# Four token norms: statistics as columns, spread by TensorE, and two row copies moved to ScalarE

## The chip, the cores and the metric

The kernel runs on one core of a Trainium2 chip. The metric is the time of one execution on the device in microseconds. Three runs of the kernel before gave 3365.01, 3369.65 and 3364.98 us, median 3365.01 us.

## What is computed

Two transformer blocks run one after the other on 512 tokens of 1024 channels, in float32. The first block has two layers: modulated RMS norm, input projection, global and window attention, short convolution, a gated merge, and an expert-choice feed-forward layer of 16 experts. Its first layer carries 256 context tokens beside the 512, so its vectors are 768 long. The second block has one layer: dilated and latent attention, a gated mix, and a feed-forward layer of width 4096 with squared ReLU. This case is about the RMS norms:

```python
def rms_norm(x, g):
    xf = x.astype(jnp.float32)
    y = xf * lax.rsqrt(jnp.mean(xf * xf, axis=-1, keepdims=True) + EPS)
    return (y * g.astype(jnp.float32)).astype(x.dtype)
...
        h = h + rms_norm(mix, norm_mix_post)
        hn = rms_norm(h, norm_mlp_pre)
        ff = jnp.square(jax.nn.relu(hn @ w_ff1)) @ w_ff2
        h = h + rms_norm(ff, norm_mlp_post)
```

## The kernel before, in words

Activations lie transposed: channels over the 128 partitions in eight tiles (`XT[:, k, :]`, k = 0 to 7), tokens along the free dimension. A norm therefore sums squares over partitions, which TensorE does: ScalarE squares tile k, and TensorE multiplies an all-ones 128x128 matrix with it, so that every partition of a PSUM tile holds the sum for each token. Float32 matmuls stand in the trace as two MATMUL and two LDWEIGHTS records each. `act_rstd` then takes Ln of that row in PSUM (L882) and Exp of -0.5 times it (L884) into the SBUF tile `rst`, 512 or 768 tokens wide. Ln and Exp stand in different tables, so a table load goes ahead of each. VectorE multiplies every tile by its gain and by `rst` (`scalar_tensor_tensor`).

Each engine has its own program in one fixed order, with semaphore waits between them. There are four PSUM tiles of 1024 float32 columns. `bank.take` hands them out in turn; `hold` and `back` keep one out of the turn. The norms that the change touches:

- **n1**, between layer 0 and layer 1, 768 tokens (L1045 reads it). TensorE adds the last squares in `pe_squares_tail` (L844): one tile by itself, then a total that GpSimd has summed, then a last pair that VectorE has summed. ScalarE has loaded the Ln table ahead (L2232). VectorE computes scaled tiles (L1045), ScalarE their rounded part (L1029), VectorE the remainder (L1038), and TensorE starts the next projection (L657).
- **n2**, between layer 1 and the second block, 512 tokens. Four sums in `pe_squares_tail`, then Ln, Exp, `dve_split_gain` (L2349 scaled tile, L2339 rounded part, L2344 remainder), and TensorE at L636.
- **no**, the norm of the mixer's output. `pe_total` adds a total of GpSimd (L873) and the last square (L876); then Ln and Exp. VectorE makes `X = X + norm` tile by tile in `dve_add_normed`: L2678 the scaled tile, L2671 the sum.
- **nf**, the norm ahead of the feed-forward layer. For each k, when tile k of X is there, TensorE transposes three of its 128-token blocks into the tiles `back` 0 to 2 (L2474) and adds the square of tile k (`pe_square`, L864). ScalarE squares tile k (L817) when the sum of tile k-2 is done. After the loop come Ln and Exp, eight transposes for `back` 3, and on VectorE three copies of `back` 0 to 2 out of PSUM (L2743), ahead of `dve_split_gain`. ScalarE copies `back` 3 later (L2637). Then the 32 units of the first feed-forward matrix run (L636) and the second (L2494), to the end.

Two forms that the change uses elsewhere are already in the kernel. The very first norm (n0) spreads columns to rows: `e.matmul(ps[...], RC[:, c:c + 1].broadcast_to([128, 128]), ident)` at L1005. The choice of experts turns a row into columns: a 128x128 slice of `rst` as the stationary operand against one column of the identity, at L1717. The end of the kernel takes Sqrt of a column and VectorE's reciprocal (L2650 to L2660, L2766).

Of the kernel before, what the change touches and what calls it, by code (L numbers as in the profile page):

```python
# [18 lines left out]
KD = 8  # L19
# [227 lines left out]
def build(nc, I, cst, cmask, crope, at, out):  # L247
    ctx = ExitStack()
    with ctx:
# [782 lines left out]
        def dve_split_mod(e, l, ks, between=None):  # L1032
            m, X = MD[l], WX[l]

# [6 lines left out]
            for k in ks:  # L1041
                if k > 1:
                    e.wait_ge(*d_xl.at(X.key, "mod", k - 2, 1))
                for w, (a, b) in enumerate(segs(T0)):
                    e.scalar_tensor_tensor(out=raw2[k % 2][:, a:b], in0=XT[:, k, a:b], scalar=A1v[:, l, 0, k, w:w + 1], in1=rst[:, a:b],  # L1045
# [118 lines left out]
        def dve_proj(e, l, norm):  # L1164
            X = WX[l]
            if l:
                e.wait_ge(*d_mod.at("mod", 3 * l, "A"))
                e.wait_ge(*n_rs.at(norm))
# [820 lines left out]
        def pe_back(e, l, p, norm=None):  # L1989
# [166 lines left out]
        def pe_experts(e, l):  # L2156
# [53 lines left out]
        def act_experts(e, l):  # L2210
# [21 lines left out]
            e.activation(sm[:, 16:17], eps[:, 0:1], ACT.Ln, bias=eps[:, 0:1]).then_inc(*n_ln.up(st, "set"))  # L2232
# [7 lines left out]
            act_rstd(e, f"n{l + 1}", KD, T, D)  # L2240
# [44 lines left out]
        def dve_experts(e, l):  # L2285
# [16 lines left out]
            dve_low(e, WX[l + 1], 0)  # L2302

# [37 lines left out]
        def dve_split_gain(e, stage, base):  # L2341
# [4 lines left out]
            for k in range(KD):  # L2346
                if k > 1:
                    e.wait_ge(*d_xl.at(stage, k - 2))
                e.scalar_tensor_tensor(out=runs(raw2[k % 2][:, 0:NX]), in0=X_(k), scalar=colB(base + k), in1=runs(rst[:, 0:NX]),  # L2349
# [55 lines left out]
        def pe_second(e):  # L2405
# [58 lines left out]
            pe_total(e, "no", KD, NX, tmp[:, 2304:2816], sqr[0])  # L2464
            pe_norm_take(e, "nf")

            def back_take(c):
                ps, when = bank.take(("back", c), c_out.at("fin", "back", 3) if c == 3 else d_out.at("fin", "back", c))
# [18 lines left out]
            for f in range(32):  # L2487
                pe_linear3(e, X2, ("f1", f), 128, NX, ("x2", "f1", f), c_ev.at("x2", "f1", f), low=(lambda k: d_xl.at("ffgain", k)) if f == 0 else None)
# [531 lines left out]
```

## Time and profile before

| what | value |
|---|---|
| median of three runs | 3365.01 us |
| the profiled execution, its own time | 3363.93 us |
| its span, first to last instruction | 3362.0 us |
| TensorE busy | 3179.4 us, 95% |
| VectorE busy | 1400.7 us, 42% |
| ScalarE busy | 1068.3 us, 32% |
| mean granted TensorE clock | 0.983 |

The span is 1.93 us shorter than the execution's own time. A clock of 1.00 is TensorE at 2.4 GHz, 0.50 at 1.2 GHz. Busy time of TensorE is modelled for the ends of matmuls, so starts are read rather than ends where many follow each other. PEld are the weight loads of TensorE.

### The profile page before, as it was taken

What the parts mean: (1) busy time and instruction counts of PE and PEld (TensorE: products, weight loads), DVE (VectorE), ACT (ScalarE), POOL (GpSimd) and SP (SyncE); (2) the same over time, 40 slices, a digit from 0 to 9 for tenths busy, and PEclk for the clock granted to TensorE, in tenths of its full rate; (3) what the DMA queues carried; (4) which work ended last, traced back from release to release, by engine and by line L of the source; (5) the groups of instructions that cost most, each with busy time, mean ns of one, the idle gap of its engine ahead of it and who ended that gap; (6) DMA issues with size and microseconds to landing.
All of it is one profiled execution on the core that took longest, in us unless ns stands there. A gap on an engine that the chain in (4) does not pass through costs nothing.

```text
span 3362.0 us, 46341 instructions
## 1 busy us (share of the span) xinstructions
PE 3179.4 (95%) x20065; PEld 2136.8 (64%) x20065; DVE 1400.7 (42%) x2110; ACT 1068.3 (32%) x1843; POOL 278.2 (8%) x221
## 2 busy tenths in 40 slices
PE   7999999999899999999999998988889999989999
PEld 6886688888334344377678873323238757868887
DVE  4476655664201011156665541211134454453333
ACT  4715632222321211165552231100022354342323
POOL 1100100211000000011000220000002020110000
PEclk9999999999899999999999998999999999999999
DMA  8240033433999998734007649999973111323332
GB/s 233 56 128 18 1 94 107 119 102 141 336 397 365 397 348 348 250 60 133 24 17 217 193 160 377 421 421 421 422 277 94 31 50 51 95 68 99 96 100 69
DMA packets 399500, 616.91 MB, mean 183 GB/s; under 512 B 99679, under 2 KB 290497, under 8 KB 374721
## 3 DMA queue, kind: packets, MB, share of 16 engines
q1 hardware_dynamic: 393616, 597.50, 50.7%
q0 software_dynamic: 5184, 15.79, 1.4%
q8 instruction: 159, 2.61, 0.3%
q10 hardware_dynamic: 496, 0.66, 0.1%
q14 instruction: 45, 0.36, 0.0%
HBM read 606.55 MB, written 7.34 MB: 183 GB/s over the span
## 4 chain that ended last, share of the span: by engine, by line
PE 79%; DMA 8%; DVE 6%; ACT 4%; issue 1%; POOL 1%; DVEq 0%; SPq 0%; ACTq 0%; POOLq 0%
PE ps L636 32%; PE ps L2110 7%; PE ps L2494 5%; PE ps L1251 4%; PE ps L2113 3%; PE ps L2146 3%; PE ps L2106 3%; PE ps L1346 3%; PE ps L689 3%; PE ps L1528 3%; PE ps L1301 3%; DMA ring<-in_w_e_up 2%; PE ps L657 2%; PE ps L2142 2%; DMA arena<-in_w_e_down 2%; DMA ring<-in_w_e_down 2%
## 5 line engine op out<-in xcount | busy, mean ns | idle before, releaser
L636 PE MATMUL ps<-xh,wh 128*128 128x512 f32 x1912 | 634.3, 370 | 26.0 <-DVE xl L2344 10.5
L636 PE MATMUL ps<-xl,wh 128*128 128x512 f32 x1912 | 626.7, 366 | 0.0
L636 PE MATMUL ps<-xh,wl 128*128 128x512 f32 x1912 | 626.0, 365 | 0.0
L609 DVE TENSOR_TENSOR wl<-ring,wh 128x1024 fp32r<-128x1024 f32 (+1 forms) x259 | 318.6, 1231 | 305.1 <-ACT wh L600 304.5
L600 ACT ACTIVATE wh<-ring 128x1024 fp32r<-128x1024 f32 (+1 forms) x259 | 271.9, 1050 | 420.2 <-PE ps L636 167.0
L636 PEld LDWEIGHTS ps<-xh,wh 128*128 128x128 f32 x1912 | 328.4, 188 | 104.8 <-issue 26.2
L636 PEld LDWEIGHTS ps<-xh,wl 128*128 128x128 f32 x1912 | 328.4, 188 | 60.3
L636 PEld LDWEIGHTS ps<-xl,wh 128*128 128x128 f32 x1912 | 328.6, 188 | 57.9 <-issue 0.5
L2110 PE MATMUL ps<-ring,arena 128*32 128x512 f32 x1344 | 177.2, 599 | 1.0 <-ACT arena L1806 0.9
L765 DVE SCALAR_TENSOR_TENSOR tmp<-ring,cs,tmp 128x512 f32<-128x512 f32 x224 | 169.2, 803 | 1.9
L2106 PE MATMUL ps<-ring,arena 128*64 128x512 f32 x696 | 158.8, 599 | 8.1 <-DMA ring<-in_w_e_up 4.8
L1262 DVE TENSOR_REDUCE sm<-ps 128x2 f32<-128x1536 f32 (+3 forms) x96 | 142.1, 1480 | 26.1 <-PE ps L1251 25.3
L2274 DVE SCALAR_TENSOR_TENSOR y<-ps,aff,y 128x1024 fp32r<-128x1024 f32 x16 | 20.5, 1284 | 304.1 <-ACT y L2203 304.1
L1251 PE MATMUL ps<-arena 64*128 64x256 f32 (+3 forms) x800 | 143.2, 442 | 2.2 <-ACT arena L2583 2.2
L1280 ACT ACTIVATE tmp<-ps,sm 128x768 f32<-128x768 f32 (+3 forms) x176 | 132.7, 762 | 36.4 <-DVE sm L1265 25.5
L1301 PE MATMUL ps<-consts,tmp 128*128 128x128 f32 x832 | 130.5, 285 | 7.7 <-ACT tmp L1280 2.2
L1301 PEld LDWEIGHTS ps<-consts,tmp 128*128 128x128 f32 x832 | 87.5, 141 | 55.4 <-issue 26.3
L1324 DVE COPY arena<-ps 128x512 f32<-128x512 f32 (+1 forms) x136 | 86.5, 655 | 80.4 <-PE ps L1301 80.3
L2106 PEld LDWEIGHTS ps<-ring,arena 128*64 128x64 f32 x696 | 48.4, 137 | 107.9 <-issue 82.0
L2203 ACT ACTIVATE y<-ps,aff 128x1024 fp32r<-128x1024 f32 x16 | 17.8, 1115 | 308.7 <-PE ps L2152 159.4
L1599 ACT ACTIVATE tmp<-ps 128x768 f32<-128x768 f32 (+1 forms) x48 | 33.9, 706 | 254.3 <-PE ps L636 254.3
L1251 PEld LDWEIGHTS ps<-arena 64*128 64x128 f32 (+1 forms) x800 | 89.3, 187 | 34.6 <-issue 26.3
(342 smaller groups left out, 4592.9 us busy)
## 6 DMA issues: line engine op xcount, KB each, us to landing
ring<-in_w_e_up SPq DMA_DIRECT2D x86, 1024.0 KB, 14.1
ring<-in_w_e_gate SPq DMA_DIRECT2D x85, 1024.0 KB, 14.1
ring<-in_w_e_down SPq DMA_DIRECT2D x82, 1024.0 KB, 14.9
ring<-in_w_in SPq DMA_DIRECT2D x112, 512.0 KB, 4.0
arena<-in_w_e_down SPq DMA_DIRECT2D x46, 1024.0 KB, 14.8
arena<-in_w_e_gate SPq DMA_DIRECT2D x43, 1024.0 KB, 13.7
arena<-in_w_e_up SPq DMA_DIRECT2D x42, 1024.0 KB, 11.3
ring<-in_w_ada SPq DMA_DIRECT2D x80, 512.0 KB, 4.3
```

What stands on the lines that cost most here:

```text
L600: e.activation(in_heads(X, u, m.WH[:, o:o + many]), heads_of(X, u, halves.aps[s], many), ACT.Copy).then_inc(*hi.up(X.key, q))
L609: e.tensor_tensor(in_heads(X, u, m.WL[:, o:o + many]), heads_of(X, u, halves.aps[s], many), in_heads(X, u, m.WH[:, o:o + many].bitcast(F32 ...
L636: i = e.matmul(ps[0:M, a:b], w[:, k, 0:M], h[:, k, a:b], start=k == 0 and p == 0, stop=k == 7 and p == 2)
L689: i = e.matmul(ps[0:M, 0:512].rearrange("p (h t) -> p h t", h=2), w[:, k, o:o + M], aside(h, k), start=k == 0 and p == 0, stop=k == kn - 1 ...
L765: e.scalar_tensor_tensor(out=ACC[w], in0=src, scalar=csv[:, k, w:w + 1], in1=ACC[w], op0=ALU.mult, op1=ALU.add).then_inc(*d_md.up("mod", g ...
L1251: x = e.matmul(ps[:, col:col + k.shape[-1]], q, k, start=first, stop=last, skip_group_check=True)
L1262: e.tensor_reduce(mx, A.units(i, A.scores(i)), AX, ALU.max).then_inc(*a_rm.up(A.stage, i))
L1280: e.activation(dst[:, u], src[:, u], ACT.Exp, bias=A.small(i, 1)[:, u:u + 1], scale=s["scale"], accum_out=A.small(i, 2)[:, u:u + 1]).then_ ...
L1301: x = e.transpose(ps[:, 128 * c:128 * c + 128], src[:, u, 128 * b:128 * b + 128], ident)
L2106: i = e.matmul(o, rows_of(1, kk, x, 0, 64), W[:, k, part], start=kk == 0, stop=kk == 7)
L2110: e.matmul(pa[64 * h + g:64 * h + g + 32, 512 * w:512 * w + 512], rows_of(0, kk, x, g, g + 32), W[:, k, 512 * h:512 * h + 512], start=kk = ...
L2494: i = e.matmul(ps[:, n:n + 512], ff_part(h, f)[c], w[:, 0, n:n + 512], start=f == 0 and p == 0, stop=f == 31 and p == 2, skip_group_check= ...
```

## The change

The sums of squares of the four norms are turned round. `pe_sums` makes the squares, 128 tokens at a time, the stationary operand and one column of ones the moving one: the sum of 128 tokens comes out as a column of PSUM, one token per partition (4 columns for 512 tokens, 6 for 768). `act_deviation` takes Sqrt of these few columns, `dve_over` the reciprocal, and `pe_over` spreads them over all partitions with the identity, 128 tokens per matmul, into the same PSUM tile. VectorE reads the factor from PSUM (`over`) in place of `rst`. The tile stays held until VectorE's last scaled tile. The table loaded ahead (L2232) is now that of Sqrt. In the second block one tile is held for both norms, and the copies of `back` 1 and 2 go from VectorE to ScalarE: `back` 1 right after the square root of nf, `back` 2 inside `act_split_gain` after its tile 1. The queue of the PSUM tiles after layer 1 is rotated by one.

```diff
             def add(src, first=False, last=False):
-                for a, b in segs(T):
-                    i = e.matmul(ps[:, a:b], ones[:, :], src[:, a:b], start=first, stop=last)
-                return i
+                return pe_sums(e, ps, T, src, first, last)
...
+        def pe_sums(e, ps, T, src, first, last):
+            for c in range(T // 128):
+                i = e.matmul(ps[:, T + c:T + c + 1], src[:, 128 * c:128 * c + 128], ones[:, 0:1], start=first and c == 0, stop=last,
+                             skip_group_check=True)
+            return i
+
+        def pe_over(e, stage, T):
+            ps = bank.of["norm", stage]
+            e.wait_ge(*d_an.at(stage, "over"))
+            for c in range(T // 128):
+                i = e.matmul(ps[:, 128 * c:128 * c + 128], RC[:, c:c + 1].broadcast_to([128, 128]), ident, start=True, stop=True)
+                if c == 3:
+                    i.then_inc(*p_n.up(stage, "over", 0))
+            if T > 512:
+                i.then_inc(*p_n.up(stage, "over", 1))
+
+        def act_deviation(e, stage, kn, T):
+            e.wait_ge(*p_n.at(stage, kn - 1))
+            e.activation(RC[:, 0:T // 128], bank.of["norm", stage][:, T:T + T // 128], ACT.Sqrt, bias=eps[:, 0:1],
+                         scale=1.0 / D).then_inc(*n_ln.up(stage))
+
+        def dve_over(e, stage, T):
+            e.wait_ge(*n_ln.at(stage))
+            e.reciprocal(RC[:, 0:T // 128], RC[:, 0:T // 128]).then_inc(*d_an.up(stage, "over"))
...
+                    if l and k == 0:
+                        e.wait_ge(*p_n.at("n1", "over", w))
+                    e.scalar_tensor_tensor(out=raw2[k % 2][:, a:b], in0=XT[:, k, a:b], scalar=A1v[:, l, 0, k, w:w + 1], in1=over[:, a:b],
...
                 pe_squares_tail(e, f"n{l + 1}", SUMMED[l], T0 - NC_ * l, norm_bufs(l), norm_total(l))
+                pe_over(e, f"n{l + 1}", T0 - NC_ * l)
...
-            normed = (n_ln.at(f"n{l + 1}"),)
+            normed = (d_y.at("gain", KD - 1) if l else d_y.at("x1", KD - 1, 1),)
             bank.start((normed, read, read, read) if l else (read, read, normed, read))
+            if l:
+                bank.queue.append(bank.queue.pop(0))
...
-            e.activation(sm[:, 16:17], eps[:, 0:1], ACT.Ln, bias=eps[:, 0:1]).then_inc(*n_ln.up(st, "set"))
+            e.activation(sm[:, 16:17], eps[:, 0:1], ACT.Sqrt, bias=eps[:, 0:1]).then_inc(*n_ln.up(st, "set"))
...
             dve_low(e, WX[l + 1], 0)
+            dve_over(e, f"n{l + 1}", T0 - NC_ * l)
...
+        def act_back(e, c):
+            e.wait_ge(*p_out.at("back", c))
+            e.activation(BACK[c], quarters(bank.of["back", c]), ACT.Copy).then_inc(*c_out.up("fin", "back", c))
...
+                if stage == "ffgain" and k == 1:
+                    act_back(e, 2)
...
-            pe_total(e, "no", KD, NX, tmp[:, 2304:2816], sqr[0])
-            pe_norm_take(e, "nf")
+            ps, when = bank.hold("no, nf", d_y.at("ffgain", KD - 1))
+            for w in when:
+                e.wait_ge(*w)
+            bank.of["norm", "no"] = bank.of["norm", "nf"] = ps
+            e.wait_ge(*l_na.at("no", KD - 2))
+            pe_sums(e, ps, NX, tmp[:, 2304:2816], True, False)
+            e.wait_ge(*n_sq.at("no", KD - 1))
+            pe_sums(e, ps, NX, sqr[0], False, True).then_inc(*p_n.up("no", KD - 1))
+            pe_over(e, "no", NX)
...
-                pe_square(e, "nf", k, KD, NX, sqr[k % 2])
+                e.wait_ge(*n_sq.at("nf", k))
+                pe_sums(e, ps, NX, sqr[k % 2], k == 0, k == KD - 1).then_inc(*p_n.up("nf", k))
+            pe_over(e, "nf", NX)
...
+                if f == 2:
+                    bank.back("no, nf")
...
-            act_rstd(e, "nf", KD, NX, D)
+            act_deviation(e, "nf", KD, NX)
+            act_back(e, 1)
...
-            e.wait_ge(*n_rs.at(stage[0]))
+            dve_over(e, stage[0], NX)
+            over = bank.of["norm", stage[0]]
+            e.wait_ge(*p_n.at(stage[0], "over", 0))
...
-            for c in range(3):
-                e.wait_ge(*p_out.at("back", c))
-                e.tensor_copy(BACK[c], quarters(bank.of["back", c])).then_inc(*d_out.up("fin", "back", c))
-            e.wait_ge(*n_rs.at("nf"))
-            e.wait_ge(*d_an.at("no", "x", 7))
-            dve_split_gain(e, "ffgain", 32)
+            e.wait_ge(*p_out.at("back", 0))
+            e.tensor_copy(BACK[0], quarters(bank.of["back", 0])).then_inc(*d_out.up("fin", "back", 0))
+            dve_over(e, "nf", NX)
+            dve_split_gain(e, "ffgain", 32, "nf")
```

## Rows read from the trace of the kernel before

**Rows 1.** Chain of waits behind the last norm: start us, us, what.
```profile
3011.31 168.88 PE ps L636 x744
```
**Rows 2.** Timeline around n1: start us, us, engine, line, operation, [idle before].
```profile
1440.53 2.36 DVE L609 TENSOR_TENSOR wl<-ring,wh 128x1024 fp32r<-128x1024 f32 x2
...
1440.60 1.56 PE L844 MATMUL ps<-hbuf,ones 128*128 128x512 f32 x4 [0.38 <-DVE hbuf L828]
...
1445.35 2.21 DVE L1045 SCALAR_TENSOR_TENSOR tmp<-arena,A,tmp 128x512 f32<-128x512 f32 x4 [2.46 <-ACT tmp L884]
...
1448.76 0.55 PE L657 MATMUL ps<-wh,xh 128*128 128x256 f32 x1 [6.61 <-DVE xl L1038]
```
**Rows 3.** Chain of waits around n2.
```profile
2496.48 3.45 PE ps L844 x8
...
2502.62 0.76 DVE tmp L2349
```
**Rows 4.** Chain of waits through norms no and nf.
```profile
2977.87 1.28 ACT L882
...
2981.83 1.42 DVE tmp L2678 x2
...
2983.99 0.87 PE ps L2474 x3
...
2986.64 0.64 PE ps L2474 x3
...
2992.47 0.86 PE ps L864 x2
...
2994.84 0.87 PE ps L864 x2
...
2998.41 0.76 DVE tmp L2349
```
**Rows 5.** Timeline of the same stretch: the last sum of no, two additions, the copies.
```profile
2977.91 1.13 PE L876 MATMUL ps<-tmp,ones 128*128 128x512 f32 x2 [0.58 <-ACT tmp L817]
...
2985.93 0.68 DVE L2671 TENSOR_TENSOR arena<-arena,tmp 128x512 f32<-128x512 f32 x1
...
2987.32 0.69 DVE L2671 TENSOR_TENSOR arena<-arena,tmp 128x512 f32<-128x512 f32 x1
...
2994.66 3.49 DVE L2743 COPY arena<-ps 128x1024 f32<-128x1024 f32 x3 [1.89 <-PE ps L2474]
```
**Rows 6.** Timeline elsewhere: one-column matmuls (L1717), a spread (L1005).
```profile
22.65 1.60 PE L1005 MATMUL ps<-consts,sm 128*128 128x128 f32 x12
...
823.65 3.66 PE L1712 MATMUL ps<-wr,mod 128*128 128x64 f32 x32
...
827.14 2.48 PE L1717 MATMUL ps<-consts,tmp 128*128 128x1 f32 x12
...
2005.51 1.00 PE L1717 MATMUL ps<-consts,tmp 128*128 128x1 f32 x8
```
**Rows 7.** By source line: Sqrt, reciprocal, a VectorE operation that reads PSUM; ns min/median/max.
```profile
L2650 ACT ACTIVATE sm<-sm,eps x3: 295/295/295, 3348.8 to 3354.2; 128x1 f32<-128x1 f32 x3
...
L2766 DVE RECIPROCAL sm<-sm x4: 153/154/154, 3350.0 to 3357.9; 128x1 f32<-128x1 f32 x4
...
L2061 DVE SCALAR_TENSOR_TENSOR arena<-ps,mod,arena x88: 739/742/752, 1038.0 to 2496.5; 128x512 f32<-128x512 f32 x88
```
**Rows 8.** Windows: length; PE, PEld, DVE, ACT, POOL busy (count); PEclk; DMA share; GB/s.
```profile
826.00:827.00 1.00, 1.00 (x11) 1.00 (x10) 0.00 (x0) 0.00 (x0) 0.00 (x0) 1.00 1.02 422
...
828.00:829.00 1.00, 1.00 (x6) 1.00 (x7) 0.00 (x0) 0.00 (x0) 0.00 (x0) 0.50 1.02 418
...
1451.00:1452.00 1.00, 1.00 (x7) 1.00 (x6) 1.00 (x3) 0.32 (x1) 0.00 (x0) 0.50 0.00 0
...
2985.00:2986.00 1.00, 1.00 (x2) 0.29 (x2) 0.96 (x3) 0.63 (x1) 0.00 (x0) 0.50 0.00 0
...
2988.00:2989.00 1.00, 1.00 (x6) 0.64 (x5) 0.96 (x3) 0.33 (x1) 0.00 (x0) 0.98 0.00 0
```

More of the change, by code:

```diff
@@ L1033, in dve_split_mod @@
             m, X = MD[l], WX[l]
+            over = bank.of["norm", "n1"] if l else rst
             def low(k):
@@ L1044, in dve_split_mod @@
                 for w, (a, b) in enumerate(segs(T0)):
-                    e.scalar_tensor_tensor(out=raw2[k % 2][:, a:b], in0=XT[:, k, a:b], scalar=A1v[:, l, 0, k, w:w + 1], in1=rst[:, a:b],
+                    if l and k == 0:
+                        e.wait_ge(*p_n.at("n1", "over", w))
+                    e.scalar_tensor_tensor(out=raw2[k % 2][:, a:b], in0=XT[:, k, a:b], scalar=A1v[:, l, 0, k, w:w + 1], in1=over[:, a:b],
                                            op0=ALU.mult, op1=ALU.mult).then_inc(*d_y.up(X.key, k, w))
@@ L1167, in dve_proj @@
                 e.wait_ge(*d_mod.at("mod", 3 * l, "A"))
-                e.wait_ge(*n_rs.at(norm))
                 dve_split_mod(e, l, range(KD))
@@ L2239, in act_experts @@
             act_high(e, WX[l + 1], 0)
-            act_rstd(e, f"n{l + 1}", KD, T, D)
+            act_deviation(e, f"n{l + 1}", KD, T)
         def dve_inner(e, l, x):
@@ L2339, in act_split_gain, with dve_split_gain @@
                 e.activation(x2.XH[:, k, 0:NX], raw2[k % 2][:, 0:NX], ACT.Copy).then_inc(*c_xh.up(stage, k))
-        def dve_split_gain(e, stage, base):
+                if stage == "ffgain" and k == 1:
+                    act_back(e, 2)
+        def dve_split_gain(e, stage, base, norm):
+            over = bank.of["norm", norm]
+            e.wait_ge(*p_n.at(norm, "over", 0))
             def low(k):
@@ L2348, in dve_split_gain @@
                     e.wait_ge(*d_xl.at(stage, k - 2))
-                e.scalar_tensor_tensor(out=runs(raw2[k % 2][:, 0:NX]), in0=X_(k), scalar=colB(base + k), in1=runs(rst[:, 0:NX]),
+                e.scalar_tensor_tensor(out=runs(raw2[k % 2][:, 0:NX]), in0=X_(k), scalar=colB(base + k), in1=runs(over[:, 0:NX]),
                                        op0=ALU.mult, op1=ALU.mult).then_inc(*d_y.up(stage, k))
@@ L2463, in pe_second @@
                 pe_linear3(e, X2, ("o", d), 128, NX, ("x2", "o", d), d_xo.at("x2", d), low=(lambda k: d_xl.at("out", k)) if d == 0 else None)
-            pe_total(e, "no", KD, NX, tmp[:, 2304:2816], sqr[0])
-            pe_norm_take(e, "nf")
+            ps, when = bank.hold("no, nf", d_y.at("ffgain", KD - 1))
[7 more added lines that the diff above has]
+            pe_over(e, "no", NX)
             def back_take(c):
-                ps, when = bank.take(("back", c), c_out.at("fin", "back", 3) if c == 3 else d_out.at("fin", "back", c))
+                ps, when = bank.take(("back", c), c_out.at("fin", "back", c) if c else d_out.at("fin", "back", c))
                 for w in when:
@@ L2613, in act_second @@
             act_square(e, "no", KD - 1, FO[:, KD - 1, :], NX, sqr, tmp[:, 2304:2816])
-            act_rstd(e, "no", KD, NX, D)
+            act_deviation(e, "no", KD, NX)
             for k in range(KD):
@@ L2635, in act_second @@
                 if f == 0:
-                    e.wait_ge(*p_out.at("back", 3))
-                    e.activation(BACK[3], quarters(bank.of["back", 3]), ACT.Copy).then_inc(*c_out.up("fin", "back", 3))
+                    act_back(e, 3)
             for f in range(2, 4):
@@ L2677, in dve_add_normed @@
                 y = raw2[k % 2][:, 0:NX]
-                e.scalar_tensor_tensor(out=y, in0=src(k), scalar=colB(base + k), in1=rst[:, 0:NX], op0=ALU.mult,
+                e.scalar_tensor_tensor(out=y, in0=src(k), scalar=colB(base + k), in1=over[:, 0:NX], op0=ALU.mult,
                                        op1=ALU.mult).then_inc(*sig.up(stage[1], "y", k))
@@ L2687, in out_low @@
                 e.tensor_tensor(x2.XL[:, d, 0:NX], MX[:, d, :], x2.XHf[:, d, 0:NX], ALU.subtract).then_inc(*d_xl.up("out", d))
-            e.wait_ge(*n_rs.at("n2"))
-            dve_split_gain(e, "gain", 16)
+            dve_split_gain(e, "gain", 16, "n2")
             dve_low(e, X2, 1)
```

## The prediction

> **What bounds the kernel now.** I read the chain of waits from its end first: behind the last norm it is one run of TensorE, 744 matmuls in 168.88 us [rows 1], followed by the second feed-forward matrix. So a microsecond that a norm gives or costs goes through to the end unless a load hides it. In the long stages TensorE has work; at the four norms it waits for the statistics. I then read the chain and the timeline at each of the four. At n1 the last sum starts at 1440.60 and lasts 1.56, VectorE begins at 1445.35, TensorE is back at 1448.76 [rows 2]. At n2 eight sum records run for 3.45 from 2496.48, and VectorE begins at 2502.62 [rows 3]. Norm no: last sum from 2977.91 to 2979.04 [rows 5], VectorE at 2981.83. Then comes a loop that the reader should look at closely: from 2983.99 to 2995.71 (2994.84 + 0.87) TensorE is the chain itself, three transposes and a sum for each of eight tiles, and VectorE begins the feed-forward input at 2998.41 [rows 4]. Last I read the granted clock in windows of 1 us [rows 8].
>
> **Prices of the new pieces.** A float32 matmul is two records.
> - A column sum has its twin in L1717. At full clock eight records took 1.00; with the last one some 0.25 long, the step is about 0.11, and I take 0.12, the step of the spread below. In layer 0, mostly at half clock, twelve took 2.48: (2.48 - 0.30) / 11 = 0.20 a record [rows 6]. So 512 tokens cost 8 records: 0.96 at full clock, 1.60 at half. With the row form they cost 0.86 [rows 4]. A weight load per 128 tokens is the bound, and it doubles with the clock.
> - A spread has its twin in L1005: twelve records in 1.60, the last 0.28 long, so a step of 0.12 [rows 6]; eight records 7 x 0.12 + 0.28 = 1.12. At half clock three 128-column transposes took 0.64, 0.213 each [rows 4], so eight records 7 x 0.213 + 0.45 = 1.94.
> - Sqrt of a column 0.295, reciprocal 0.154 [rows 7]. Six columns instead of one: between 0.15 and 0.30 for either, since they cost nearly nothing beside the start; I take 0.30 and 0.15.
> - VectorE with the factor in PSUM as third operand is not shown. With PSUM as first operand the same operation takes 0.742 [rows 7]; the SBUF form stands on the chain at 0.76 [rows 3]. I take no difference; between ends of 0 and 0.05 per tile.
> - Hops between engines, by the gaps in these rows: 0.03 into ScalarE, 0.10 into VectorE, 0.04 into and out of TensorE. From the end of the last sum to VectorE that makes 0.03 + 0.30 + 0.10 + 0.15 + 0.04 + spread + 0.05 = 0.67 + spread: 1.8 at full clock, 2.6 at half. Before, it was 3.19 at n1 (1442.16 to 1445.35) [rows 2] and 2.70 at nf (2995.71 to 2998.41) [rows 4].
>
> **What decides is the clock.** From 823.65 TensorE runs 32 records with 64 columns each and then the one-column records of L1717, without a gap [rows 6]. Its busy share in the windows is 1.00 throughout, and still the granted clock goes from 1.00 (2.4 GHz) in 826 to 827 to 0.50 (1.2 GHz) in 828 to 829 [rows 8]. What the engine did before the fall was dense work with few columns. In the loop of nf the clock is 0.50 at 2985 to 2986 and comes back at 2988 while transposes alternate with 512-column sums, and is 0.98 afterwards [rows 8]. The change takes those 512-column sums out of all four places and leaves one column per record. I therefore expect that the clock, once it has fallen behind norm no, does not come back before the loop is over.
>
> **The sum, part by part.**
> - n1: all three sums of this stage now have one column per record, so I let the clock fall during the last one: between 1.57 and 2.5, take 2.1, end 1442.7. VectorE is in L609 until 1442.89 (1440.53 + 2.36) [rows 2], which hides the square root. Chain 0.67 and a spread at half clock 1.94: VectorE at 1445.3 against 1445.35. Value 0.0, ends -1.1 (full clock throughout) and +0.5.
> - n2: four sums in a row on the path. 32 records x 0.12 + 0.14 = 4.0 against 3.45 [rows 3]: +0.5 at full clock, and up to +0.6 more if the clock falls in them. Then 0.67 and a spread of 1.12 to 1.94, 1.8 to 2.6, against 2.7 (2499.93 to 2502.62): -0.9 to -0.1. Value +0.3, ends -0.4 and +1.0.
> - no: the last sum ends near 2979.0, Sqrt waits for its table until 2979.15 (2977.87 + 1.28) [rows 4]. VectorE begins at 2979.15 + 0.64 + 1.12 = 2980.9, or 2981.7 at half, against 2981.83. Value -0.5, ends -0.9 and -0.1.
> - The loop: TensorE enters it 2.16 behind VectorE as before. A round at half clock is three transposes x 0.213 + 8 x 0.20 = 2.24; VectorE gives a tile every 1.39 (2985.93 to 2987.32) [rows 5], so TensorE stays the bound. Eight rounds are 17.9, with the last record 18.0, against 11.7 now: +6.3. The squares of ScalarE wait two rounds behind and are not late.
> - From the loop's end to VectorE: 2.6 against 2.7, -0.1. The two copies that leave VectorE ran from 2994.66 for 3.49 in all [rows 5], ending 0.26 before VectorE's start, hidden by Ln and Exp. Left there they would be late now; so moving them gives 0 and avoids a stall. On VectorE a copy takes 1.16 (3.49 / 3). On ScalarE, that of `back` 1 lies in its wait for reciprocal, spread and first scaled tile (2.3 to 3.1). That of `back` 2 lies between two tiles that come 1.39 apart, and might push the next rounded tile by 0 to 0.5; VectorE has a scaled tile (0.76) to do meanwhile, so I take 0. The copy of `back` 0 ends about 0.7 before the reciprocal can start; if it were late, all that follows would be.
> - The later eight transposes for `back` 3 take 1.7 at half clock between the spread and the first L636, which comes some 2.2 behind VectorE's start, after the same order of operations as in norm no: just covered; the cover gone, 0.3. The L636 of the first unit run at VectorE's pace at either clock: three take 3 x 0.227 (168.88 / 744) = 0.68 [rows 1], at half 1.36, below 1.39.
> - Held tile and rotated queue: every tile taken is freed one unit (24 x 0.227 = 5.4) or more before it is asked for: 0. The last table load (Sqrt, at the end) goes; ScalarE waits there for TensorE anyway: 0. The first attention of the second block now has to load Exp, before VectorE has the maxima of the first scores that ScalarE waits for: 0, or 1.28 with that cover gone.
>
> Sum: 0.0 + 0.3 - 0.5 + 6.3 - 0.1 = +6.0. The profiled execution took 3363.93 (span 3362.0 and 1.93 around it), so 3369.9. The median of the runs is 1.08 above it: 3371.0. The 32 units behind, and the weights' loads, whose slots come free by VectorE, only move along.
>
> **The rivals.**
> - The clock holds (faster). TensorE has fewer and shorter idle gaps than now: the spread cuts the 4.95 us in front of the loop (2979.04 to 2983.99) into 0.8 and 2.2. If being busy is what keeps it, every spread and the loop run at full clock. A round is 3 x 0.12 + 0.96 = 1.32, below VectorE's 1.39. n1 gives 1.1, n2 0.5, no 0.9; the loop ends about 1.3 earlier and the way out gives 0.9, together 2.3 for the pair. Sum -3.9: 3360.0, in the median 3361.1. For it: the short gaps. Against it: 826 to 829, where busy 1.00 did not hold the clock. The Trainium skill, page "TensorE: Matmul & The Clock Gate", section "What's actually happening", says that the gate follows how busy TensorE has lately been; by the busy share this rival would win, and the trace disagrees with that reading (busy share 1.00, clock 0.50).
> - The clock is low for only part of the loop, or weights load faster at half clock than L1717 shows. With four rounds at VectorE's pace and four at 2.24 the loop costs 1.39 x 4 + 8.96 + 0.1 = 14.6, +2.9; the sum +2.6: 3367.6 in the median. For it: the clock before rose inside the loop. Against: the wide sums that stood before that rise are gone.
> - Slower yet. At n1, TensorE is back at 1448.76 and still at 0.50 up to 1452 [rows 8]: 3.2 us at half clock cost it 1.6 there. If the clock, already low since the sums, comes back one such stretch later, it costs 1.6 more; with n1, n2 and no at their upper ends (+0.5, +0.7, +0.4 over my values) the sum is 6.0 + 3.2 = +9.2: 3374.2. It decides from the point where the return of the clock lies behind 1452 in that stage.
> - The change does not drop the loads: if a Copy behind Sqrt wanted its own table, 1.28 would stand ahead of the first rounded tile at four places: +5. Square behind Sqrt shares it at the kernel's end, so I give this little.
>
> **How the numbers follow.** The forecast has 0.72, the clock that holds 0.13, the half way case 0.09, the slower ones 0.06. The range runs from 3361.0 (the clock that holds) to 3374.0. The forecast's own range by its ends is 3368.8 to 3373. Within 0.2% (6.7 us) is what a measurement here can tell from no change. The forecast lies 0.7 inside that bound with some 1.5 of spread, so a third of it falls beyond: slower 0.72 x 0.33 + 0.06 = 0.30. Faster by over 0.2% needs 2.8 more than the fast rival has: 0.05. Same 0.65.
>
> **What would show it.** Right: the granted clock 0.50 from about 2982 until past 3000; rounds of 2.2 us in the loop; L2349 of the feed-forward norm starting near 3004 counted from an unmoved start. VectorE's operations with PSUM at 0.74 to 0.75 would confirm that price, and the copies on ScalarE with no waiter their cover. Wrong: rounds of 1.3 to 1.4 us with the clock at 1.00 there. If the one-column records step much below 0.20 at half clock, the mis-sized term is the loop.

## The result and the profile after

| | before | after |
|---|---|---|
| median of 15 runs | 3364.95 us | 3373.78 us |
| lowest to highest | 3362.58 to 3369.65 | 3370.74 to 3376.50 |
| profiled execution, its span | 3363.93, 3362.0 | 3374.22, 3372.3 |
| mean granted TensorE clock | 0.983 | 0.981 |

The kernel became slower by 8.8 us: ratio 1.0026, 95% interval 1.0019 to 1.0033. The forecast said 3371.0 with a range of 3361.0 to 3374.0, so the sign is the forecast's and the time lies in the range, but only by 0.2 us. It lies 0.8 above the range that the forecast gave for itself (3368.8 to 3373), and the chance for slower by over 0.2% was only 0.30. All medians in this document are over every execution; one of nf_rows (4970.51 us) and one of exp_ahead (6449.24 us) are counted in the medians of these two kernels and left out of their ratios.

**Norm n1.** Timeline of the kernel after, in the columns of [rows 2]:
```profile
1441.92 1.92 PE L860 MATMUL ps<-ones,hbuf 128*128 128x1 f32 x12 [0.43 <-DVE hbuf L828]
1443.88 0.27 ACT L876 ACTIVATE sm<-ps,eps 128x6 f32<-128x6 f32 x1 [1.11 <-PE ps L860]
1444.42 2.93 PE L868 MATMUL ps<-consts,sm 128*128 128x128 f32 x12 [0.58 <-DVE sm L881]
1446.60 2.31 DVE L1071 SCALAR_TENSOR_TENSOR tmp<-arena,A,ps 128x512 f32<-128x512 f32 x4 [2.23 <-PE ps L868]
1450.12 0.55 PE L657 MATMUL ps<-wh,xh 128*128 128x256 f32 x1 [2.77 <-DVE xl L1062]
```
The last sum starts 1.32 later than in [rows 2] (1441.92 against 1440.60): work ahead of it is the same in both kernels, so this is drift between executions. VectorE starts 1.25 later. What n1 itself did is the difference, -0.07. (From the last square to the first L657, as in the table of experiments, it is +0.04.)

**Norm n2.** Chain of the kernel after (start us, us, what), beside [rows 3]:
```profile
2498.83 4.58 PE ps L860 x32
...
2503.96 2.09 PE ps L868 x8
...
2506.08 0.76 DVE tmp L2386
```
The sums take 4.58 where the rows took 3.45. From their end to VectorE it is 2.67, as before (2.69). TensorE's clock in windows of this stretch (us, busy of PE, PEld, DVE, ACT and POOL with their instructions, PEclk, DMA share, GB/s) falls in the middle of the sums:
```profile
2500.00:2501.00 1.00, 1.00 (x11) 1.00 (x10) 0.69 (x1) 1.00 (x2) 0.00 (x0) 0.98 0.40 74
2501.00:2503.00 2.00, 2.00 (x11) 2.00 (x11) 1.23 (x2) 0.23 (x1) 0.00 (x0) 0.50 0.89 336
```

**First attention of block 2.** ScalarE's timeline after:
```profile
2619.07 1.28 ACT L1305 ACT_TABLE_LOAD   x1 [4.49 <-DVE sm L1290]
2620.36 0.90 ACT L1305 ACTIVATE tmp<-ps,sm 128x768 f32<-128x768 f32 x1
```
and of the same place before:
```profile
2615.71 0.90 ACT L1280 ACTIVATE tmp<-ps,sm 128x768 f32<-128x768 f32 x1 [4.50 <-DVE sm L1265]
```
Read the releaser in brackets: the load of Exp's table did not use the 4.49 us of idle time. It was issued only once VectorE's maxima (L1290) had come, so all its 1.28 is on the path. And the next run of 13 score matmuls became slower. The chain after, then before:
```profile
2619.07 1.28 ACT L1305
...
2624.17 3.69 PE ps L1276 x13
```
```profile
2619.42 2.16 PE ps L1251 x13
```
TensorE waits longer for the exponentials, and its clock, 1.00 until 2622, is 0.50 at 2624 to 2626. From ScalarE's copy ahead of it (2613.56 and 2610.19) to the end of these 13 matmuls it is 14.30 after and 11.39 before: +2.9 where the prediction had 0.

**Norms no and nf.** Chain of the kernel after, beside [rows 4]:
```profile
2982.80 1.28 ACT L876
...
2984.09 0.27 ACT sm L876
...
2984.62 1.18 PE ps L868 x8
...
2985.82 1.41 DVE tmp L2728 x2
...
2987.97 0.88 PE ps L2518 x3
2988.85 1.56 PE ps L860 x8
2990.42 0.74 PE ps L2518 x3
2991.16 1.50 PE ps L860 x8
...
3004.60 1.51 PE ps L860 x8
...
3006.66 2.09 PE ps L868 x8
...
3008.78 0.76 DVE tmp L2386
```
From the start of the table load to VectorE: 3.02, before 3.96 [rows 4] (2977.87 to 2981.83), so -0.94. The loop runs from 2987.97 to 3006.11, 18.1 against 11.7. After its first round, each is 0.74 + 1.50 = 2.24. The clock:
```profile
2984.00:2985.00 1.00, 0.38 (x3) 0.38 (x4) 0.18 (x1) 0.35 (x2) 0.00 (x0) 1.00 0.00 0
...
2996.00:2997.00 1.00, 1.00 (x7) 1.00 (x6) 0.73 (x2) 0.00 (x0) 0.00 (x0) 0.50 0.00 0
3002.00:3003.00 1.00, 1.00 (x7) 1.00 (x5) 0.00 (x0) 0.34 (x1) 0.00 (x0) 0.50 0.00 0
...
3010.00:3011.00 1.00, 0.07 (x1) 0.00 (x0) 0.93 (x3) 0.97 (x3) 0.00 (x0) 1.00 0.00 0
```
From the loop's end to VectorE it is 2.67 against 2.70 (2995.71 to 2998.41), with the factor read from PSUM at 0.76 for the first scaled tile, as from SBUF. The L636 run starts at 3021.63, 10.3 later than in [rows 1], and the span is 10.3 longer: what comes behind only moved along, as the prediction said. Of the 10.3, the stages named here account for 10.1. The rest is drift between them, which nearly cancels: +1.3 ahead of n1 and -1.3 between the attention and norm no.

### The profile page after: what moved, and what is told of

The parts are those of the page before. It is cut to its first block, busy times and chain, and to the rows that moved or that the text cites. A ratio compares the mean times of both kernels' runs of the same rounds, so it can differ in the third digit from the quotient of the medians.

```text
span 3372.3 us, 46623 instructions
## 1 busy us (share of the span) xinstructions
PE 3194.5 (95%) x20209; PEld 2160.3 (64%) x20209; DVE 1398.6 (41%) x2112; ACT 1058.1 (31%) x1836; POOL 278.8 (8%) x221
## 4 chain that ended last, share of the span: by engine, by line
PE 79%; DMA 8%; DVE 6%; ACT 4%; issue 1%; POOL 1%; SPq 0%; DVEq 0%; ACTq 0%; POOLq 0%
PE ps L636 32%; PE ps L2136 7%; PE ps L2542 5%; PE ps L1276 4%; PE ps L2139 3%; PE ps L2172 3%; PE ps L2132 3%; PE ps L1371 3%; PE ps L689 3%; PE ps L1553 3%; PE ps L1326 3%; DMA ring<-in_w_e_up 2%; PE ps L657 2%; PE ps L2168 2%; DMA arena<-in_w_e_down 2%; DMA ring<-in_w_e_down 2%
## 5 line engine op out<-in xcount | busy, mean ns | idle before, releaser
L636 PE MATMUL ps<-xh,wh 128*128 128x512 f32 x1912 | 634.2, 370 | 21.3 <-DVE wl L609 6.6
L636 PE MATMUL ps<-xh,wl 128*128 128x512 f32 x1912 | 627.4, 366 | 0.0
L636 PE MATMUL ps<-xl,wh 128*128 128x512 f32 x1912 | 626.5, 366 | 0.0
L636 PEld LDWEIGHTS ps<-xh,wh 128*128 128x128 f32 x1912 | 328.7, 188 | 100.9 <-issue 19.7
L636 PEld LDWEIGHTS ps<-xh,wl 128*128 128x128 f32 x1912 | 328.2, 188 | 60.3
L636 PEld LDWEIGHTS ps<-xl,wh 128*128 128x128 f32 x1912 | 327.9, 188 | 58.8 <-issue 0.5
```

What stands on the lines that cost most here:

```text
L636: i = e.matmul(ps[0:M, a:b], w[:, k, 0:M], h[:, k, a:b], start=k == 0 and p == 0, stop=k == 7 and p == 2)
```

## The experiments

The runs of the kernel before beside them had a median of 3364.95 (for after), 3363.44 (nf_rows to copies_back) and 3364.02 (all later ones). The last columns are read from the chain of each profiled execution, in us. n1: from the start of ScalarE's last square (L837) to the first L657. n2: from ScalarE's `y` to VectorE's first scaled tile. att: from ScalarE's copy ahead of the first attention (2610.19 before, 2613.56 after) to the end of its second 13 score matmuls. no: from VectorE's copy of the last tile to the first back transpose. loop: from there to ScalarE's statistic of nf.

| kernel | median | ratio [95%] | n1 | n2 | att | no | loop |
|---|---|---|---|---|---|---|---|
| before | 3364.95 | | 10.05 | 15.67 | 11.39 | 7.49 | 11.75 |
| after | 3373.78 | 1.0026 [1.0019, 1.0033] | 10.09 | 17.55 | 14.30 | 6.54 | 18.16 |
| nf_rows | 3367.31 | 1.0010 [1.0002, 1.0019] | 10.49 | 15.68 | 14.00 | 7.46 | 12.51 |
| filler | 3382.86 | 1.0060 [1.0047, 1.0073] | 10.50 | 15.99 | 13.86 | 7.50 | 28.39 |
| exp_ahead | 3372.11 | 1.0024 [1.0013, 1.0035] | 10.16 | 14.79 | 11.39 | 6.54 | 18.16 |
| copies_back | 3374.36 | 1.0033 [1.0020, 1.0046] | 11.25 | 17.46 | 12.67 | 6.54 | 18.15 |
| after_again | 3375.18 | 1.0030 [1.0018, 1.0043] | 10.22 | 16.56 | 13.98 | 7.46 | 18.16 |
| warm | 3369.18 | 1.0016 [1.0007, 1.0025] | 10.04 | 17.65 | 14.30 | 7.93 | 14.27 |
| n2_rows | 3369.91 | 1.0021 [1.0012, 1.0030] | 10.74 | 15.66 | 11.39 | 6.54 | 18.16 |
| sqrt_rows | 3370.47 | 1.0020 [1.0011, 1.0029] | 12.82 | 16.32 | 11.39 | 8.94 | 11.98 |
| nf_only | 3369.74 | 1.0018 [1.0009, 1.0027] | 10.05 | 15.66 | 11.39 | 7.50 | 18.15 |
| mix | 3365.47 | 1.0001 [0.9992, 1.0010] | 10.50 | 16.41 | 11.39 | 7.47 | 12.51 |
| no_only | 3362.90 | 0.9997 [0.9988, 1.0006] | 10.05 | 16.45 | 13.03 | 6.54 | 12.02 |
| n1_rows | 3371.29 | 1.0023 [1.0014, 1.0032] | 10.05 | 16.63 | 14.01 | 7.46 | 18.16 |

An interval is 2 to 4 us to either side, so differences of 1 or 2 us between two kernels are read from the chains, not from the medians. A chain is that of one execution only, and not always a typical one: the profiled execution took 3370.65 in mix and 3371.53 in nf_rows, 5.2 and 4.2 above their medians.

after_again is the changed kernel measured once more, as the measure for warm, n2_rows and sqrt_rows. Expected was +8.8 us over the kernel before, with anything from +7 to +11 as the same. It came out at +11.2 by the medians and +10.1 by the ratio, an interval of +6 to +14. So a comparison with after_again alone makes a variant look 1.3 us (ratios) to 2.4 us (medians) better than one with the first measurement.

### nf_rows: the sums in the loop as rows again
```diff
-                pe_sums(e, ps, NX, sqr[k % 2], k == 0, k == KD - 1).then_inc(*p_n.up("nf", k))
-            pe_over(e, "nf", NX)
+                e.matmul(ps[:, NX:2 * NX], ones[:, :], sqr[k % 2][:, 0:NX], start=k == 0, stop=k == KD - 1).then_inc(*p_n.up("nf", k))
...
-            act_deviation(e, "nf", KD, NX)
+            e.wait_ge(*p_n.at("nf", KD - 1))
+            e.activation(rst[:, 0:NX], bank.of["norm", "nf"][:, NX:2 * NX], ACT.Ln, bias=eps[:, 0:1], scale=1.0 / D).then_inc(*n_ln.up("nf"))
+            e.wait_ge(*n_ln.at("nf"))
+            e.activation(rst[:, 0:NX], rst[:, 0:NX], ACT.Exp, scale=-0.5).then_inc(*n_rs.up("nf"))
...
```


> The changed kernel (median 3373.8 us; 3365.0 before) with norm nf alone in the row form again: 512-column sums in the loop, Ln and Exp of a row behind it; all else as changed. Theory A (the clock follows how many columns TensorE streams): the loop starts at half clock, gets the full clock back inside, and takes 11.7 to 13 us in place of 18.1; about 3368. Rival B (the loop is slow since the idle time ahead of it took the clock, and the form of the sums has no part in that): 0.50 to the end of the loop, 8 rounds of some 2.35 us, 3374 or more.

Chain of its loop (a round is the three transposes and the sum, L2529):
```profile
2993.43 0.64 PE ps L2519 x3
2994.07 1.71 PE ps L2529 x2
...
2998.50 0.33 PE ps L2519 x3
2998.83 0.86 PE ps L2529 x2
```
The loop starts at 0.50 just as in the changed kernel, and after two rounds the clock is back (0.91 in the window 2996 to 2998, 1.00 behind). The loop is 12.5. The form of the sums inside the loop decides whether the clock returns; the time came down from +8.8 to +3.4 (0.0010 x 3364).

### filler: a wide matmul added to each round
```diff
+                e.matmul(ps[:, 640:1024], ones[:, :], sqr[k % 2][:, 0:384], start=False, stop=False, skip_group_check=True)
                 pe_sums(e, ps, NX, sqr[k % 2], k == 0, k == KD - 1).then_inc(*p_n.up("nf", k))
```


> The changed kernel with work added: in each round of the nf loop one more float32 matmul of 384 columns (ones against the squares) into unused columns of the held PSUM tile; its result is read by nobody. Theory A: the wider matmuls bring the clock back inside the loop; rounds 3.5 us at half clock for the first one or two and then 1.96 (1.32 + 2 x 0.32) at full clock: loop 17 to 18.5 us although it does more, total 3373 to 3374.5. Rival B (clock independent of the columns): every round 2.24 + 1.28 = 3.5 us, loop 28 us, 3384.

The product of the added matmul is not used. Chain of one round (L2528 is the filler):
```profile
2994.77 0.74 PE ps L2518 x3
2995.51 1.28 PE ps L2528 x2
2996.79 1.50 PE ps L860 x8
```
The clock stayed at 0.50 through all eight rounds, 3.52 each after the first, and 1.28 a round was added on the path. So 384 wide columns beside the one-column records did not bring it back; here the theory's number failed and the other came. What nf_rows and this show together: with the one-column records gone the clock came back, with wide work added to them it did not. Why the one and not the other is open: nf_rows changed two things at once, the width of the sums and their number (two records a round in place of eight), and no run separates them.

### warm: wide work ahead of the loop
```diff
             pe_sums(e, ps, NX, tmp[:, 2304:2816], True, False)
+            e.matmul(ps[:, 640:1024], ones[:, :], FO[:, 5, 0:384], start=False, stop=False, skip_group_check=True)
...
             pe_over(e, "no", NX)
+            e.matmul(ps[:, 640:1024], ones[:, :], FO[:, 7, 0:384], start=False, stop=False, skip_group_check=True)
+            e.matmul(ps[:, 640:1024], ones[:, :], FO[:, 7, 0:384], start=False, stop=False, skip_group_check=True)
+            e.matmul(ps[:, 640:1024], ones[:, :], FO[:, 7, 0:384], start=False, stop=False, skip_group_check=True)
```


> The changed kernel, with four useless matmuls of 384 columns (the same constant weights, added into a part of the held tile that nobody reads) in TensorE's idle time ahead of the loop of nf's sums: one between the two sums of no, three between no's spread rows and the first back transposes. Theory A: it is the form of the work inside the loop (matmuls of one column) that costs the clock. Then the loop may begin at 1.00, but falls to 0.50 within some rounds: rounds of about 1.5 first, 2.24 later, the loop 15 to 17 long, 1 to 3 us under the changed kernel. Rival C: the idle time before the loop (0.74 before no's spread, 2.19 after it) took the clock, and the loop would hold it if it began with it: eight rounds of 1.3 to 1.5, the loop 10.5 to 12, 6 to 7 us under the changed kernel. If the four matmuls delay the start of the loop, that shows as a later first back transpose and is taken off.

Chain of its loop, with parts left out:
```profile
2985.55 1.28 PE ps L2511 x2
...
2988.21 0.33 PE ps L2522 x3
2988.54 0.83 PE ps L860 x8
...
2993.53 0.47 PE ps L2522 x3
2993.99 1.73 PE ps L860 x8
2995.72 0.74 PE ps L2522 x3
2996.47 1.50 PE ps L860 x8
```
and the clock:
```profile
2988.00:2990.00 2.00, 2.00 (x18) 1.75 (x16) 1.96 (x4) 0.90 (x2) 0.00 (x0) 1.00 0.00 0
...
2993.00:2994.00 1.00, 1.00 (x9) 0.82 (x8) 0.96 (x3) 0.63 (x1) 0.00 (x0) 0.85 0.00 0
2994.00:2996.00 2.00, 2.00 (x10) 2.00 (x11) 1.96 (x4) 0.69 (x2) 0.00 (x0) 0.50 0.00 0
```
This is the cleanest row of the case. The loop begins at 1.00, four rounds run at 1.16 to 1.39, TensorE has no gap, and in the fifth the clock falls under one-column work. The rival that blamed the idle time would have had 10.5 to 12 in all; the theory said 15 to 17 and it was 14.3, so the right kind with a smaller size: more rounds passed before the fall than expected. The idle time is not free of blame: with it filled, 3.9 of the loop's 6.4 go. Its column "no" is longer by 0.5 than with a spread at the same clock (7.46), since the fillers delay the first transposes. By the chain warm is thus some 3.4 us under a changed kernel with the same spread. Its time is 6.0 under after_again by the medians and 4.7 by the ratios, 3.4 under the first measurement by the ratios: the time alone would fit the rival's 6 to 7 as well as the theory's 1 to 3, and it is the clock and the rounds that decide.

### nf_only: one norm in columns
```diff
+                if stage in ('n1', 'n2'):
+                    for a, b in segs(T):
+                        i = e.matmul(ps[:, a:b], ones[:, :], src[:, a:b], start=first, stop=last)
+                    return i
                 return pe_sums(e, ps, T, src, first, last)
...
-            act_deviation(e, "no", KD, NX)
+            act_rstd(e, "no", KD, NX, D)
```


> Norms n1, n2 and no as in the kernel before (rows, Ln and Exp); only nf in columns, with the two copies on ScalarE. Theory A by its own place: the loop of nf takes 17.9 to 18.1 where it took 11.7, all of its rounds 2.24 at 0.50, and the end of nf is as long as before: 6.3 us over the kernel before, and no Exp load ahead of the first attention of block 2. If the loop was only so slow because columns of no came right before it (rival G), the clock in it comes back after some rounds: 2 to 4 us over the kernel before.

Its loop starts at half clock after a norm no in rows (2983.49), and a round of it is:
```profile
2985.92 0.74 PE ps L2532 x3
2986.66 1.50 PE ps L864 x8
```
The loop is 18.15, that of the changed kernel to 0.01. The time is 6.1 us (0.0018 x 3364) over the kernel before, against 6.3 expected. The columns of no don't matter to it, so rival G falls. nf alone accounts for some two thirds of the loss.

### exp_ahead: the Exp load moved into idle time
```diff
+            e.activation(sm[:, 46:47], eps[:, 0:1], ACT.Exp, bias=eps[:, 0:1]).then_inc(*n_ln.up("exp set"))
             e.wait_ge(*d_o.at("ra", 11))
             act_attention(e, AD)
```


> The changed kernel with a one-column Exp on ScalarE behind the last copy of the values, before the first attention of the second block, so that the Exp table is there when the first scores come. Theory A: in the changed kernel the load stands behind the wait and on the chain (1.28 us), and the longer idle time of TensorE costs the clock there (1.5 us more): together 1.3 to 2.9 us less, 3371 to 3372.5. Rival: the load was hidden and the shift of 2.9 us there is chance: no change, 3373.8.

ScalarE's timeline:
```profile
2611.69 1.28 ACT L2591 ACT_TABLE_LOAD   x1
...
2616.18 0.90 ACT L1305 ACTIVATE tmp<-ps,sm 128x768 f32<-128x768 f32 x1 [2.89 <-DVE sm L1290]
```
One dummy element in front makes the load fall into the idle time. The attention is 11.39 again, as before, with 13 scores at 2.16. That is 2.9 less than in the changed kernel; the times (1.0024 against 1.0026) can't show it: their intervals overlap nearly whole, and 2.9 can't be told from nothing by them.

### n2_rows: n2 as before
```diff
-            act_deviation(e, f"n{l + 1}", KD, T)
+            if ('col', 'row')[l] == "row":
+                act_rstd(e, f"n{l + 1}", KD, T, D)
...
+            else:
+                act_deviation(e, f"n{l + 1}", KD, T)
```


> The changed kernel, with the norm n2 as it was: sums as rows of 512 columns, Ln and Exp on ScalarE, VectorE reading the factors from SBUF. Exp is then ScalarE's last function before the first attention of block 2, so its load there goes too. Theory: n2 in columns costs about 1.8 (the sums' tail +1.1 at the lower clock, the stage before them +0.8 at the lower clock, the end to VectorE 0.0), and the Exp load stands on the path, +1.28: 3.1 us under the changed kernel. Rival D: what the two profiles showed around n2 and the attention beside the load (+0.8 and the slower 13 score matmuls, +1.5) is chance, as the clock's phase is: 1.1 + 1.28 = 2.4 us under. Rival E: both belong to the change: 1.8 + 1.28 + 1.5 = 4.6 us under. The chain tells more than the times: the 13 score matmuls at 2.16 or 3.69, the load on it or not.

The load goes, the 13 scores take 2.16, n2 is 15.66: by the chain 1.9 + 2.9 = 4.8 less than the changed kernel, which is rival E's size. The times don't decide: n2_rows is 5.3 under after_again by the medians, 3.0 by the ratios, and only 1.7 under the first measurement by the ratios, all with overlapping intervals. The other rows of the table temper it too. Of the seven chains that have the load, six lose 2.5 to 2.9 at the attention and one, copies_back, exactly the 1.28. Of the seven without it six are at 11.39 and no_only is at 13.03, a fall of the clock with no load at all. So the 1.28 is the load's always, and the slower scores are a fall that the load makes likely. n2 is 14.79 to 17.65 in its eight chains with columns (mean 16.54), 15.66 to 16.45 in the five with rows (mean 15.97): +0.6 on the mean.

### n1_rows, mix and no_only
The edits are of the same kind: n1 back to Ln and Exp; n2 and nf back; all but no back. These three and nf_only ran on another chip than after_again.

> The changed kernel with n1 alone as before (rows, Ln and Exp). Theory: n1 in columns costs nothing (0.0 by the prediction, -0.1 by the two profiled executions): the time of the changed kernel, +8 to +11 us over the kernel before. Rival H: the +1.3 that the changed kernel was late ahead of n1, and more behind it, comes from n1's columns (the clock's phase passed on): 1.5 to 3 us under the changed kernel, +6 to +8 us over the kernel before.

> n1 and no in columns as changed, n2 and nf in rows as before, the two copies on ScalarE. Theory: nothing that costs is left, and the end of no keeps its gain (the sum for it was -0.9 by the trace of the changed kernel), n1 is worth 0: 1 us under the kernel before, -2 to +1. Rival H: the parts don't add, and something of +2 or more stays that neither taking n2 nor taking nf back alone has shown (a later phase of the clock upstream, as the +1.3 ahead of n1 in the profiled execution of the changed kernel): +1 to +3 us.

> Only no in columns, n1, n2 and nf in rows as before, the two copies on ScalarE. Theory: -0.9 for no, +0.1 for the copy that now stands ahead of ScalarE's first split after nf: 0.8 us under the kernel before, within what can be told from none. Against mix it tells the price of n1 in columns: 0 by the theory.

n1_rows is +7.3 us over the kernel before by the medians and +7.7 by the ratio. That is in the rival's band (+6 to +8) and below the theory's (+8 to +11), and 3.9 under after_again, with overlapping intervals (1.0014 to 1.0032 and 1.0018 to 1.0043): by its time alone the theory missed and the rival is not excluded. By the chains, n1 is 10.05 in all four with rows (Ln and Exp) and 10.04 to 11.25 in nine with columns, mean 10.44: +0.4. And n1 starts as early with columns (1436.37 in n2_rows) as with rows (1436.50 in n1_rows), so the +1.3 ahead of n1 is not owed to its columns. mix, with the columns where they cost least, equals the kernel before (1.0001): no hidden remainder of +2 or more is seen, though the interval reaches to +3.4. no_only has the shortest chain into the last run; its L636 starts 0.5 before that of [rows 1]:
```profile
2978.06 1.28 ACT L880
...
2979.88 1.17 PE ps L872 x8
...
2981.08 1.40 DVE tmp L2745 x2
```
Its time is 1.1 us under the kernel before, 0.9997 [0.9988, 1.0006], as expected and not to be told from no change. It is the best version found, and it is not shown to beat the kernel before.

### sqrt_rows: Sqrt and reciprocal without columns
```diff
+            e.activation(rst[:, 0:T], bank.of["norm", stage][:, at:at + T], ACT.Sqrt, bias=eps[:, 0:1],
+                         scale=1.0 / D).then_inc(*n_ln.up(stage))
...
+            e.reciprocal(rst[:, 0:T], rst[:, 0:T]).then_inc(*d_an.up(stage, "over"))
```


> All four norms with their sums as rows of 512 or 768 columns again, as before the change, but ScalarE takes one Sqrt of the row and VectorE its reciprocal, in place of Ln and Exp; the one-column Exp ahead of the first attention of block 2, and the two copies on ScalarE as changed. Theory: the loop of nf is as before (11.7), and of the end of a norm the load of Exp (1.28) falls out with Ln and Exp exchanged for Sqrt (0.64) and a reciprocal of 512 columns. If that takes as long as the other operations of VectorE on 512 columns (0.61 to 0.76), each of no, nf and n2 ends 1.2 us sooner than before and n1 1.1 (0.97 for 768 columns): 4 to 5 us under the kernel before. Rival F: the reciprocal of a row is several times dearer than another operation of its length (the one column of the norm at the end took 0.154, which is no measure): at 2.0 us each nothing is gained, at 3 us each the kernel is 4 us over the kernel before.

Norm nf of this kernel:
```profile
3000.40 0.70 ACT tmp L885
...
3001.12 3.36 DVE tmp L890
```
VectorE's reciprocal of 128x512 takes 3.36, and at n1 that of 768 takes 4.96, against 0.18 for four columns. Rival F holds: with 512 columns Ln, load and Exp together took 2.6 and Sqrt and reciprocal 4.1, +1.4 at each of three norms; at n1, with 768, 3.1 became 5.9, +2.8. Together that is some +7.1, and the measurement has +6.7 (0.0020 x 3364). This kernel holds exp_ahead's element too, so its attention is 11.39. This is what the columns are good for: they take the reciprocal from 512 elements a partition to 4.

### copies_back: the row copies on VectorE again
```diff
-            e.wait_ge(*p_out.at("back", 0))
-            e.tensor_copy(BACK[0], quarters(bank.of["back", 0])).then_inc(*d_out.up("fin", "back", 0))
+            for c in range(3):
+                e.wait_ge(*p_out.at("back", c))
+                e.tensor_copy(BACK[c], quarters(bank.of["back", c])).then_inc(*d_out.up("fin", "back", c))
```


> The changed kernel with the copies of back 1 and back 2 on VectorE again, all three in a row ahead of the reciprocal of nf. Theory A: three copies of 1.16 end about 1.3 us after the square root, so the reciprocal and all behind it are 1.3 us later: 3375.1. Rival: hidden, 3373.8; moving them was worth nothing.

VectorE's timeline:
```profile
3005.90 3.49 DVE L2789 COPY arena<-ps 128x1024 f32<-128x1024 f32 x3 [7.47 <-PE ps L2516]
3009.31 0.17 DVE L881 RECIPROCAL sm<-sm 128x4 f32<-128x4 f32 x1
```
ScalarE's Sqrt started at 3007.83 and took 0.26, and the reciprocal would have been ready at 3008.13; it begins some 1.2 later, behind the third copy. So the move of the copies is worth 1.2 as long as the factor is in columns. The time (3374.36) lies between the theory's 3375.1 and the rival's 3373.8 and decides nothing; the chain does. With Ln and Exp the copies were hidden ([rows 5]: they end 0.26 before VectorE goes on), so there the move gains nothing.

## Why the prediction was right, and which term was not

The last column is the mean over all chains above that have the new form, less the mean over those with the old one. For the attention the form is the Exp load on the chain or not. sqrt_rows counts for neither form at n1, n2 and no; warm is left out of no, warm and filler out of the loop.

| term | predicted | the two profiles | mean over the chains |
|---|---|---|---|
| n1 | 0.0 | -0.1 | +0.4 |
| n2 | +0.3 | +1.9 | +0.6 |
| first attention of block 2 | 0 | +2.9 | +2.3 |
| no | -0.5 | -0.9 | -0.5 |
| loop of nf | +6.3 | +6.4 | +6.0 |
| way out of nf | -0.1 | -0.1 | -0.1 |
| sum | +6.0 | +10.1 | +8.7 |

- **How near the forecast was.** The mechanism and its place were right. The size was +6.0 where +8.8 and, in after_again, +10.1 came (by the ratio). That 3373.78 still lies in the range is luck: the upper end, 3374.0, was taken from the slower rival, whose mechanism did not come, and the median of after_again, 3375.18, lies above it.
- **The loop** carries the forecast, and came as worked out: at half clock 1.50 for eight one-column records (predicted 1.60) and 0.74 for three transposes (0.64), 2.24 a round; counted from an unmoved start of norm no, VectorE's first scaled tile came at 3003.85, as named (near 3004). Two errors of 0.10 cancelled in it. So did two on the way from the sums to the factor: 0.58 without the spread (predicted 0.67) and 2.09 for the spread at half clock (1.94). Against all row loops, 11.75 to 12.51, the price is +6.0. nf_rows and warm show the cause that the prediction named, and warm corrects it: with one-column sums in the loop the clock fell even without idle time (warm), with row sums it came back in spite of it (nf_rows). The idle time in front decided how early the slow rounds began.
- **The faster rival** (the clock holds as long as TensorE is busy) is refuted by the loops: in warm the clock fell in a stretch with busy share 1.00. The half-way rival is what warm made artificially (its loop 14.27, the rival's 14.6), not what the change does.
- **no.** The chance of the spread's clock is seen: 1.18 in five of ten chains (warm apart), 2.09 in five; hence 6.54 or 7.46. The value of -0.5 between the ends -0.9 and -0.1 was the right kind of answer.
- **n2.** The price of the sums, +0.5 and up to +0.6 more at half clock, was found whole: 4.58 - 3.45 = +1.13. The rest of the +1.9 lies in the projection ahead of the sums, and by the spread of the chains that is the clock's chance.
- **The term that failed** is the last one of the prediction's list: the first attention "now has to load Exp, before VectorE has the maxima of the first scores that ScalarE waits for: 0, or 1.28 with that cover gone". The idle time was there, 4.49 us of it, but the load was put behind the wait, not ahead of it. And where the full 1.28 is on the path, TensorE idles by as much longer, after which the clock fell in six of seven chains for 1.2 to 1.6 more. The prediction had the bound of 1.28 and left it out of both the value and the forecast's own range, whose upper end would have been 3374.3 with it. What the runs showed in its place is +2.9 between the two profiles and +2.3 on the mean.
- **The slower rival** had +9.2, nearly the time that came, but by other means: the clock came back at n1 within 1453 to 1454 (0.97), before within 1452 to 1453 (0.98), which is the 1.3 of drift, and n1 did not cost 1.6 more.
- **The copies**: on ScalarE no one waits for them when the factor is in columns; left where they were they would have cost 1.2 by copies_back. Behind Ln and Exp that of `back` 1 stands on the chain ahead of ScalarE's first rounded tile (0.91 in nf_rows and no_only), yet it delays nothing: L636 comes 15.58 behind the loop's end in nf_rows, 15.60 in the kernel before.

What stays open: whether the 3.9 us between n1_rows and after_again are more than scatter, and the sum over single terms, since +8.7 stands beside the two measurements of the changed kernel (+8.8, and +10.1 by 1.0030) but each has 2 to 4 us of interval. And it stays open which property of the one-column records, their number or their width, keeps the clock low.

## What to carry to other kernels

Before making the moving side of a TensorE step narrow to save another engine's time, look at what stands around it: in the tight loop the narrow form went with half the clock for 18 us, while at the three norms that stand alone it cost +0.4, +0.6 and -0.5. Even there its gain is not shown: no_only, the best version, can't be told from the kernel before. When an activation function is exchanged, follow every table that it used to leave behind to its next user: a load isn't hidden because the engine is idle. Read in the trace whether it stands ahead of the wait, as at norm no, or behind it, as at the attention, where one dummy element ahead of the wait hid it. Bounds that are written down for a lost cover belong in the sum or the range.

## What was not expected of the hardware

- VectorE's reciprocal costs by the element: 0.18 us for 128x4, 3.36 for 128x512, 4.96 for 128x768 (1.60 for 256 elements a partition more), where its other float32 operations on 128x512 take 0.6 to 0.76. The Trainium skill, page "VectorE: DVE Perf Modes", section "First, the fixed hardware budget", describes it as an iterative divide with a repeat count of 8; the trace agrees in kind, with four to six times the time of another operation of this length.
- Ln and Exp cost a load each in a row-form norm: nf_rows has one of 1.28 from 3001.63, ahead of Ln and hidden by the loop, and one of 1.28 from 3004.00, between Ln and Exp, on the path. The Trainium skill, page "ScalarE: Activation LUTs", section "Table sets: the hidden batching unit", says that one set holds both, so that Ln and then Exp need a single load. The trace disagrees, with two loads, and the measurement decides; which set each of them brought is not shown. With a single load the way out of a norm in rows would, by an estimate from these rows, be 1.28 shorter, and the columns would have had less to offer.
- One and the same program has a clock that falls or doesn't at the same place in different executions: in after no's spread took 1.18 and n2 17.55, in after_again, the same kernel, 2.09 and 16.56. Over kernels that do the same work there n2 took 14.79 to 17.65, and the last square ahead of n1 started between 1436.4 and 1440.9 in kernels that do the same work up to there. The position of one stage in one profile is good to some 2 us; its length compares better, within such a spread.
- ScalarE's table loads are placed differently from place to place: at norm no the load (2982.80 to 2984.08) starts 0.02 after the last square, while the sums that Sqrt waits for still run (until 2983.89), at the attention behind the wait.
